# Half-wise gated sums, diagonal turns in pairs, and a new order of the second mixer in a two-block transformer kernel

## The reference

```python
def odd_mixer(t, w_in, ...):
    proj = t @ w_in                      # 704 columns: 256 | 256 | 128 | 64
    y_c = s5_ssm(proj[..., :o1], ...)    # state-space part, 16 groups of 64 states
    y_d = mla_attention(proj[..., o1:o2], proj[..., o2:o3], proj[..., o3:], q_norm, w_uq, kv_norm, w_ukv, cos, sin)
    return jnp.concatenate([y_c, y_d], axis=-1) @ w_out

# inside mla_attention
    q = (rmsnorm(c_q, q_norm) @ w_uq)    # 256 -> 6 heads x 192
    kv = (rmsnorm(c_kv, kv_norm) @ w_ukv)  # 128 -> 6 heads x 256
```

```python
def branch_merge(ya, yb, ga, gb, w_pa, w_pb, w_o):
    merged = jax.nn.sigmoid(ga) * (ya @ w_pa) + jax.nn.sigmoid(gb) * (yb @ w_pb)
    return merged @ w_o
```

## Time and profile before

| | before |
|---|---|
| median of 3 runs | 2024.42 us |
| profiled execution | 2029.02 us, span 2027.2 us |
| granted TensorE clock, mean | 0.979 |
| PE busy | 1893.8 us (93%) |
| POOL busy | 1349.0 us (67%) |
| ACT busy | 929.4 us (46%) |
| DVE busy | 721.2 us (36%) |

### The profile page before, as it was taken

One profiled execution on the slowest core, in us unless ns is written; L12 is line 12 of the kernel. 1 busy time (PEld: TensorE's weight loads), 2 busy tenths in 40 slices (PEclk: granted clock), 3 DMA queues, 4 the chain that ended last, 5 costly groups with the idle time before them and its releaser, 6 DMA issues.

```text
span 2027.2 us, 28312 instructions
## 1 busy us (share of the span) xinstructions
PE 1893.8 (93%) x9582; PEld 1503.2 (74%) x9582; DVE 721.2 (36%) x1296; ACT 929.4 (46%) x1458; POOL 1349.0 (67%) x780
## 2 busy tenths in 40 slices
PE   7977899988989999998999999999999899989997
PEld 5656788775668878677888787777887787768886
DVE  1375433256521115444211345442112545442112
ACT  5444444343454445464444545544444435644442
POOL 5405899550478887656888794477887684468884
PEclk9998899989989999999999999999999999999999
DMA  7657555556676554434675452245765452245552
GB/s 260 224 196 257 161 186 186 172 173 221 220 249 191 185 174 145 156 115 135 178 215 185 147 178 91 90 140 161 201 200 165 133 169 92 91 140 168 185 186 72
DMA packets 257208, 344.32 MB, mean 170 GB/s; under 512 B 33376, under 2 KB 153056, under 8 KB 257120
## 3 DMA queue, kind: packets, MB, share of 16 engines
q1 hardware_dynamic: 243328, 337.13, 51.9%
q10 hardware_dynamic: 13792, 6.03, 1.7%
HBM read 342.03 MB, written 1.05 MB: 169 GB/s over the span
## 4 chain that ended last, share of the span: by engine, by line
PE 86%; DVE 6%; ACT 3%; DMA 2%; issue 2%; SPq 0%; POOL 0%; ACTq 0%; DVEq 0%
PE bank L1929 24%; PE bank L1931 24%; PE bank L1930 24%; PE bank L2000 3%; PE bank L2459 2%; PE bank L2449 2%; PE bank L2476 2%; PE bank L2011 1%; PE bank L1979 1%; DMA raw<-in_w_mod 1%; PE bank L2166 1%; ACT wh L662 1%; PE bank L2246 1%; DVE arena L1347 1%; PE bank L2441 0%
## 5 line engine op out<-in xcount | busy, mean ns | idle before, releaser
L641 POOL TENSOR_TENSOR wl<-raw,wh 128x1024 fp32r<-128x1024 f32 x300 | 726.0, 2430 | 104.2 <-ACT wh L800 97.9
L1929 PE MATMUL bank<-wh,xh 128*128 128x512 f32 (+2 forms) x1746 | 692.9, 397 | 39.6 <-issue 17.6
L626 POOL TENSOR_TENSOR wl<-raw,wh 128x512 fp32r<-128x512 f32 (+2 forms) x238 | 321.3, 1350 | 547.4 <-ACT wh L662 512.5
L1931 PE MATMUL bank<-wl,xh 128*128 128x512 f32 (+2 forms) x1746 | 678.5, 389 | 0.0
L1930 PE MATMUL bank<-wh,xl 128*128 128x512 f32 (+2 forms) x1746 | 676.8, 388 | 0.0
L800 ACT ACTIVATE wh<-raw 128x1024 fp32r<-128x1024 f32 x270 | 286.5, 1062 | 454.9 <-PE bank L1931 427.5
L1929 PEld LDWEIGHTS bank<-wh,xh 128*128 128x128 f32 x1746 | 332.0, 190 | 115.7 <-issue 45.5
L1931 PEld LDWEIGHTS bank<-wl,xh 128*128 128x128 f32 x1746 | 331.7, 190 | 67.8
L1930 PEld LDWEIGHTS bank<-wh,xl 128*128 128x128 f32 x1746 | 332.3, 190 | 62.4 <-issue 0.7
L662 ACT ACTIVATE wh<-raw 128x1024 fp32r<-128x1024 f32 (+2 forms) x268 | 274.9, 1047 | 217.6 <-PE bank L1931 166.4
L627 POOL TENSOR_TENSOR wl<-raw,wh 128x512 fp32r<-128x512 f32 (+2 forms) x238 | 317.8, 1335 | 0.0
(11 more groups left out here) (316 smaller groups left out, 1660.2 us busy)
## 6 DMA issues: line engine op xcount, KB each, us to landing
raw<-in_w_ffn_in SPq DMA_DIRECT2D x264, 256.0 KB, 3.0
raw<-in_w_in SPq DMA_DIRECT2D x224, 256.0 KB, 2.9
raw<-in_w_mod SPq DMA_DIRECT2D x192, 256.0 KB, 3.8
raw<-in_w_ffn_out SPq DMA_DIRECT2D x132, 256.0 KB, 3.0
raw<-in_l_w_gate SPq DMA_DIRECT2D x88, 256.0 KB, 3.6
raw<-in_l_w_up SPq DMA_DIRECT2D x88, 256.0 KB, 4.3
raw<-in_l_w_down SPq DMA_DIRECT2D x88, 256.0 KB, 2.9
raw<-in_l_w_in SPq DMA_DIRECT2D x48, 256.0 KB, 4.3
```

The lines of the kernel that those rows point to most:

```text
L626: nc.gpsimd.tensor_tensor(wl[:, s, 0:h], raw[:, s, 0:h], words(wh)[:, s, 0:h], ALU.subtract)
L641: nc.gpsimd.tensor_tensor(wl[:, s, :], raw[:, s, :], words(wh)[:, s, :], ALU.subtract)\
L1929: mm(dst, x_hi, w_hi, start=first, stop=False, skip_group_check=True)
L1931: return mm(dst, x_hi, w_lo, start=False, stop=last, skip_group_check=True)
```

## The change

Four edits, here in the order of the program on the chip.

1. **Diagonal turns in pairs.** `rows_turn` went through all eight channels of token tile 0 and then of tile 1. Now the order is (pair, tile): (0,0), (1,0), (0,1), (1,1), (2,0), (2,1), (3,0), (3,1). All seven norms.
2. **Second mixer.** The two latents are handled apart: squares, root, rows, turn and split of `c_q` come before tile 1 of `in1`, those of `c_kv` behind two chunks of `uq`. Six modulation chunks are placed behind the three `uq` and three `ukv` chunks, one each; three stay in front of the attention and move behind its first six turns.
3. **Attention steps.** The scan step goes ahead of the maximum of unit u+2.
4. **Gated sum by halves.** The first half is summed and turned while tile 1 of `pb` is evacuated; ACT writes `xh` straight from PSUM, DVE only the remainder.

```diff
-    plan.gemm("uq", a["l1_w_uq"], [384] * 3)
-    plan.gemm("ukv", a["l1_w_ukv"], [512] * 3)
-    plan.modulation("mod1_rope", 1, w_mod[1], 9)
+    each = {n: (1, w_mod[1]) for n in range(3)}
+    plan.gemm("uq", a["l1_w_uq"], [384] * 3, modulated=each)
+    plan.gemm("ukv", a["l1_w_ukv"], [512] * 3, modulated=each)
+    plan.modulation("mod1_rope", 1, w_mod[1], 3)
...
 (ACT, second mixer)
+            for b in range(3):
+                evac_b(b)
+            latent_root(0)
+            evac_b(3)
+            evac_latent(0)
+            act.wait_ge(ssm_ut, 1)
+            nc.scalar.activation(uT1, ...).then_inc(ssm_uev, 1)
+            latent_root(1)
+            tail("in1")
+            hi_until(plan.tiles["uq"][1][2][0][0] + 1)
+            evac_latent(1)
             act.wait_ge(c_in, 32)
             nc.scalar.activation(cz[1], cz[1], ACT.Copy, scale=-1.0).then_inc(c_neg, 1)
-            tail("ukv")
             for i in range(3):
+                hi_until(plan.tiles["uq"][i][2][0][0] + RING)
                 act.wait_ge(chunk_used, plan.tiles["uq"][i][2][-1][0] + 1)
...
 (ACT, gated sum)
-                    if pair >= 2:
-                        act.wait_ge(xt_split, split_at[f"m_{name}"] + pair - 1)
-                    nc.scalar.activation(xf[:, pair % 2, :], turn_banks(f"m_{name}")[pair][:, :], ACT.Copy).then_inc(m_ev, 1)
+                    nc.scalar.activation(xh[:, 2 * pair:2 * pair + 2, :],
+                                         turn_banks(f"m_{name}")[pair][:, :].rearrange("p (a b) -> p a b", a=2),
+                                         ACT.Copy).then_inc(m_ev, 1)
...
 (DVE, attention steps of the second mixer)
-                if u + 2 < 2 * MH:
-                    mla_top(u + 2)
                 next(ssm)
                 if u % 4 == 3:
                     next(ssm)
+                if u + 2 < 2 * MH:
+                    mla_top(u + 2)
...
 (DVE, gated sum: gated(branch, i) multiplies a tile, mixed(i) adds a half, m_split(pair) writes xl)
+                gated(0, 0)
+                gated(0, 1)
+                gated(1, 0)
+                mixed(0)
+                gated(1, 1)
+                m_split(0)
+                mixed(1)
+                m_split(1)
                 gate_spread(f"o_{name}", gain)
                 gate_diagonal(f"ffn_{name}", s, l, 5)
                 norm_scale(s, l, 4)
+                m_split(2)
+                m_split(3)
...
 (PE, rows_turn)
-                    for t in range(TT):
+                    for pair, t in ((0, 0), (1, 0), (0, 1), (1, 1), (2, 0), (2, 1), (3, 0), (3, 1)):
                         pe.wait_ge(norm_xn, TT * n + t + 1)
-                        for k in range(KD):
+                        for k in (2 * pair, 2 * pair + 1):
...
 (PE, second mixer)
+            latent_turn(0)
             pe.wait_ge(b_ev, 4)
             turn(ut_bank, lambda i, t: proj[:, t, i * P:i * P + P], ssm_ut)
+            tile_chunk("in1", 1, 1)
             modulate("mod1_lat")
             pe.wait_ge(ssm_uev, 1)
             pe.wait_ge(b_ev, 8)
             drive(0)
+            x_ready("lat1", 1)
+            latent_chunk("uq", 0)
+            latent_chunk("uq", 1)
+            latent_turn(1)
             drive(1)
+            pe.wait_ge(evac, plan.tile_no["uq"] + 1)
+            latent_chunk("uq", 2)
+            drive(2)
...
 (PE, gated sum)
+                m_turns(0)
                 gate_rows(f"o_{name}")
+                pe.wait_ge(evac, plan.tile_no[f"o_{name}"] - 2)
+                for part in range(4):
+                    x_ready(f"m_{name}", part + 1)
+                    tile_chunk(f"o_{name}", 0, part)
+                    if part == 0:
+                        m_turns(1)
```

138 lines of the change are left out of this document (73 added, 65 removed).

## The result

| | before | after |
|---|---|---|
| median of the runs | 2025.01 us (4 runs, 2022.0 to 2030.69) | 2002.55 us (4 runs, 2001.95 to 2004.69) |
| ratio | | 0.9887, 95% interval 0.987 to 0.9905 |
| profiled execution | 2029.02 us | 2001.95 us |
| granted clock, mean | 0.979 | 0.980 |

A forecast was written before the change was run, and what follows sets the result against it. PE bounds the kernel, busy 1893.8 of 2027.2 us, so an edit is worth the PE idle time it takes. From the median of 2024.4 us, 11.1 + 7.5 + 7.4 + 1.7 = 27.7 us less gives 1997 us; range 1988 to 2010.

The forecast's parts named there:

- the upper bound: Gated sum, three places: all idle time and the shorter queue behind it are won, 4.0 us a place, 12 in sum.
- what is late next is pair 2: Gated sum: the split of pair 2 stands behind DVE's copy of the gate row, with 1.4 us to spare.
- The catch with POOL at the second SwiGLU: Second SwiGLU's turn: DVE's earlier cast meets an earlier POOL instruction, 0.2 us won in place of 1.36; 0.8 taken.
- The lower bound of 3.0: Turns in pairs: the four sites with POOL at work give nothing, leaving 3.0 us for the seven turns.
- The wait ahead of the third `uq` chunk: Second mixer: a new PE wait of 3.6 us, as ACT's `wh` half stands behind the second latent's copy and the negation.
- the first two waits: Second mixer: PE's waits for scaled latents (1.5 us) and their split (2.8 us) go; 0.7 of 4.3 us gain is left.
- The modulation chunks behind six turns: Second mixer: three modulation chunks cover 1.0 of PE's 1.1 us wait for the last copy before the attention.
- 1.3 us gained behind the removed waits: Second mixer: the clock, granted at 0.59 over 3 us behind the waits for modulation chunks, stays full, 1.3 us won.
- The rivals of 2001 and 2003 us: POOL: first block's four turns give nothing, 2001 us, chance 0.14; halves: PE still waits at the second half, 2003 us, 0.09.
- the signs against me: PE waits for weights (POOL or DMA) right behind the gated sums, or mixer waits for modulation chunks, would show the forecast wrong.

The follow-up runs named there:

- the quarters run: The changed kernel with POOL computing each `wl` half of a chunk outside the SwiGLUs in four instructions, not two: 2094.49 us, ratio 1.0323.

## Why the prediction was right, point by point

The forecast was 1997 us, the time 2002.55, inside the range of 1988 to 2010. The single terms were off in both directions, and that they cancel in part is luck.

- **Gated sum by halves: 11.1 forecast.** 3 x 4.23 = 12.7 us in the stretch itself, more than the 12 of the upper bound, with all idle time gone as written. The step that failed is that nothing behind it would change: "what is late next is pair 2" looked at the same stage, not at the adds behind `w_o`, which met POOL. They gave back 0.8 us a place against undisturbed executions, 0.6 on the mean of the ruler. The longer wait ahead of the turns then cost another 0.65 us a place by the clock under them: 12.7 - 1.8 - 2.0 = 8.9 us net. That the adds' two SBUF sources make the turn late is shown by the run with one in PSUM. That the clock is lower behind a late turn rests on the counts above and was not tested by itself.
- **Turns in pairs: 7.5 forecast.** In the second block 3 x 1.2 = 3.6 us, like with like, for 3.0 forecast. In the first block 5.3 us up to the first product, for 4.5 forecast, but only 2.1 us are left at the 25th: 5.7 us in all. The step that failed is that I followed the gain to the first product only, and not to the `wh` and `wl` of the chunk behind it. The catch with POOL at the second SwiGLU was real (7.23 and 7.25 us against 6.2 to 6.3, in two of eight profiles, with casts of 1.4 us), but it makes no difference at the 25th product (13.0 us in both cases). The lower bound of 3.0, all casts blocked, was not met for its reason.
- **Second mixer: 7.4 forecast**, about 6.4 us to the first scores. The wait ahead of the third `uq` chunk was forecast at 3.6 and measured at 4.12 us, so that of the 4.3 us of the first two waits nothing was left, where I counted 0.7. The modulation chunks behind six turns covered 0.3 us of the last wait and not 1.0. What was mis-sized most is the clock: I counted 1.3 us gained behind the removed waits (the earlier trace rows alone gives 0.41 x 3.00 = 1.2) and nothing lost behind the new one, which lost 1.2 to 1.8 us. This term carried only for the old place.
- **Attention steps: 1.7 forecast**, 3.0 us by the ruler. The profile of the changed kernel, with 0.8 us, had shown less than most.
- **Sum.** 8.9 + 5.7 + 6.4 + 3.0 = 24.0 us, forecast 27.7. Timed were 22.5 us, with an interval of 19 to 26, and 21.4 us (medians). The 2 us between are within the scatter. The rivals of 2001 and 2003 us are nearer to the measured time than my forecast. The first had the effect almost right, since the first block's turns gave 2.1 us of 4.5, but not the cause: the first product came earlier by the full size at three places of four, and what took the gain back were waits for weights. The second is not what happened: no wait at the second half stood.
- **Profile against median.** Of the 27.1 us between the two profiled executions, 7.0 lie in the first SwiGLU behind its first product: one vector instruction of 10.66 us there; in the thirteen other profiles only the quarters run has its like in that stretch (17.14 us). I had the 4.6 us by which that profile lay above its median, and did right to count from the median.
- **Would show it.** Most signs came: no idle time at the gated sums, the first copy out of the banks 1.9 us behind the first turn of context 0 in place of 4.0, 0.16 us of waiting behind that turn, no DMA wait in the mixer and one wait of 3 to 4 us (4.1). Two came in part: the scores were earlier by 4.1 us in the two profiles and by about 6.4 in the ruler, not 7, and DVE still waits for scores in the attention, five times and not nine. Of the signs against me, waits for weights right behind the gated sums did not come; they came behind the first block's turns, where I had not named them.

## What to carry to other kernels

When work on one engine moves earlier, look at what it now lies beside, one stage further than the edit, and follow the gain past the next chunk of weights before you count it. A wait of 4 us on PE cost 1.2 to 1.8 us more than itself here; count the clock behind new waits as well as behind removed ones. Give a vector operation on the critical path one source in PSUM while POOL has a long unbroken row of work, and judge an edit of a few us by stretches between landmarks over several profiles rather than by one difference of totals.

## What was not expected of the hardware

- A DVE instruction with both sources in SBUF beside a row of POOL instructions without a gap can be kept out until the row ends: 8.72, 10.38, 25.41 and 31.33 us for instructions that take 0.7 to 1.4 us elsewhere. The one of 10.66 us got its turn inside a row, while POOL went on behind it. The add behind `w_o` was kept out at four of the thirty places in the ten profiles that have it with two SBUF sources, the quarters aside (8.63, 8.69, 8.72 and 10.38 us); in the profile of the changed kernel it took 1.0 to 1.7 us. A square of 0.9 us in a norm of the second block took 9.3 us in six of thirteen profiles. With one source in PSUM the adds behind `w_o` took 0.69 us, 12 of 12 in the profile above.
- A cast is kept out too, though it has one source: one `xh` cast of the second block took 3.9 to 4.1 us in twelve of thirteen profiles, 0.42 us at most other places.
- Cutting POOL's instructions from 1.35 us to 0.77 us, two into four, made the kernel some 85 us slower.
- Part of the scatter between executions comes from it: behind `w_o` the turn came at 14.8 to 15.4 us, or at 17.4 to 17.5 where an add had been kept out, in three of fifteen places of kernels with the old order.
